# A hybrid decoder layer: operand splits behind the score blocks, chunk states from a bank of their own, the silu at its head's end, and the merge's first products in another order

## What is computed

```python
# mixer A: 12 query heads in 3 groups over 4 key/value heads; windowed, dilated softmax attention
oa = dilated_attention(qa, ka, va)              # groups weighted by their softmax denominators
# mixer B: gated linear attention, 4 heads, chunk by chunk
o_t = q_t S_t ;  S_t = diag(a_t) S_{t-1} + k_t^T v_t
ob = rmsnorm(ob, gn_b) * silu(rb)
# merge
y = sigmoid(ga) * (oa @ w_proj_a) + sigmoid(gb) * (ob @ w_proj_b)
x = x + y @ w_out
# channel mixer
x = x + (silu(h2 @ w_ffn_gate) * (h2 @ w_ffn_up)) @ w_ffn_down      # h2 = rmsnorm(x)
```

## Time and profile before

| what | value |
|---|---|
| median of three runs | 1862.59 us (1861.71 to 1868.87) |
| the profiled execution | 1860.7 us, of which the span is 1859.0 us |
| TensorE busy | 1790.2 us, 96% of the span |
| VectorE, ScalarE, GpSimd busy | 1081.9, 702.9, 487.1 us |
| mean granted TensorE clock | 0.994 of full |
| memory traffic | 150.88 MB read, 44.45 MB written |

### The profile page before, as it was taken

One profiled execution on the slowest core, in us unless ns is written; L12 is line 12 of the kernel. 1 busy time (PEld: TensorE's weight loads), 2 busy tenths in 40 slices (PEclk: granted clock), 3 DMA queues, 4 the chain that ended last, 5 costly groups with the idle time before them and its releaser, 6 DMA issues. The chain is left out here.

```text
span 1859.0 us, 27056 instructions
## 1 busy us (share of the span) xinstructions
PE 1790.2 (96%) x9188; PEld 1518.4 (82%) x9188; DVE 1081.9 (58%) x1928; ACT 702.9 (38%) x1598; POOL 487.1 (26%) x578
## 2 busy tenths in 40 slices
PE   6999999999999999999988999989999999999999
PEld 6888887988887888888876888868888888878887
DVE  4362452643734949485766554596555555556786
ACT  5333243243333335353535213453333333334443
POOL 2010001110114424150602000006665556520120
PEclk9999999999999999999999999999999999999999
DMA  7211321413222111111117323312323223278764
GB/s 204 88 42 59 93 86 50 127 63 86 74 74 79 49 35 49 32 45 45 39 63 249 100 70 114 134 65 97 107 91 122 91 99 105 85 266 311 249 223 168
DMA packets 169294, 196.35 MB, mean 106 GB/s; under 512 B 9552, under 2 KB 119472, under 8 KB 168704
## 3 DMA queue, kind: packets, MB, share of 16 engines
q1 hardware_dynamic: 156816, 163.13, 27.4%
q0 software_dynamic: 6128, 21.74, 3.6%
q10 hardware_dynamic: 6272, 10.49, 1.5%
HBM read 150.88 MB, written 44.45 MB: 105 GB/s over the span
## 5 line engine op out<-in xcount | busy, mean ns | idle before, releaser
L2236 PE MATMUL bank<-act_hi,w_hi 128*128 128x512 f32 x568 | 230.6, 406 | 3.9 <-DVE act_lo L1870 3.6
L2238 PE MATMUL bank<-act_hi,w_lo 128*128 128x512 f32 x568 | 224.1, 395 | 0.0
L2237 PE MATMUL bank<-act_lo,w_hi 128*128 128x512 f32 x568 | 223.6, 394 | 0.0
L2236 PE MATMUL bank<-ca,wq 128*128 128x512 f32 x528 | 206.3, 391 | 7.6 <-DVE wq L1981 5.3
L2238 PE MATMUL bank<-ca,wq 128*128 128x512 f32 x528 | 205.5, 389 | 0.0
L2237 PE MATMUL bank<-ca,wq 128*128 128x512 f32 x528 | 205.5, 389 | 0.0
L2236 PE MATMUL bank<-w_hi,act_hi 128*128 128x256 f32 (+1 forms) x576 | 180.7, 314 | 2.2 <-DVE act_lo L1553 2.2
L2238 PE MATMUL bank<-w_hi,act_lo 128*128 128x256 f32 (+1 forms) x576 | 177.4, 308 | 0.0
L2237 PE MATMUL bank<-w_lo,act_hi 128*128 128x256 f32 (+1 forms) x576 | 177.3, 308 | 0.0
L1537 DVE TENSOR_TENSOR w_lo<-w_raw,w_hi 128x1024 fp32r<-128x1024 f32 x38 | 46.1, 1224 | 154.1 <-ACT w_hi L1002 154.1
L2236 PEld LDWEIGHTS bank<-act_hi,w_hi 128*128 128x128 f32 x568 | 108.5, 191 | 27.4 <-DVE act_lo L1870 4.2
(11 more groups left out here) (357 smaller groups left out, 4222.0 us busy)
## 6 DMA issues: line engine op xcount, KB each, us to landing
w_raw<-in_w_in SPq DMA_DIRECT2D x60, 512.0 KB, 4.1
rawd<-in_w_ffn_down SPq DMA_DIRECT2D x99, 256.0 KB, 5.1
rx<-y_scratch SPq DMA_DIRECT2D x77, 256.0 KB, 4.2
wr<-in_w_ffn_gate SPq DMA_DIRECT2D x11, 1024.0 KB, 5.3
wr<-in_w_ffn_up SPq DMA_DIRECT2D x11, 1024.0 KB, 5.3
y_scratch<-sq SPq DMA_DIRECT2D x11, 1024.0 KB, 4.3
y_scratch<-yq SPq DMA_DIRECT2D x33, 256.0 KB, 2.0
gate_scratch<-gbuf ACTq DMA_DIRECT2D x32, 256.0 KB, 2.0
```

What stands on the lines that cost most here:

```text
L2236: pe.matmul(ps, lhs_hi, rhs_hi, start=first, stop=False, skip_group_check=onto)
L2237: pe.matmul(ps, lhs_hi, rhs_lo, start=False, stop=False, skip_group_check=onto)
L2238: return pe.matmul(ps, lhs_lo, rhs_hi, start=False, stop=last, skip_group_check=onto)
```

## The change

It does five things.

1. **Splits behind score units** (blocks 8 to 15 of each attention head): ScalarE's cast goes behind the block's copies and exponentials, VectorE's subtraction and `merge_mul` behind its score units.
2. **Silu at its head's end**: `act_silu(h)` runs at s=11 of its own head, ahead of that step's jobs; its table is loaded at s=7. ScalarE's loop over the heads is written out in full.
3. **The last chunks**: the products for the states of chunks 4 to 7 go to bank 1, `dve_last_m` updates the state without waiting for ScalarE's square, and chunk 7's product, which nobody reads, is left out.
4. **Splits of the mixers' outputs**: three casts of oa move to s=10 of the last head, the fourth and the cast of tile 2 to its end; one subtraction follows each chunk, and tile 2's comes right after them. The first product waits slice by slice.
5. **The merge's first step**: all four products with w_pa come first, then the four with w_pb; the second half goes to banks 5, 4, 6 and 7, so `down` has one more wait (at d=2).

```diff
@@ banks of the merge @@
-    def mix_base(it, f):
-        return 4 if (it, f) == (NC_IT - 1, 0) else 0
+    def mix_banks(it, f, xh):
+        if (it, f) == (0, 1):
+            return 5 + xh, (4, 7)[xh]
+        b = 4 if (it, f) == (NC_IT - 1, 0) else 0
+        return b + xh, b + 2 + xh
@@ act_head_a @@
-                for k in HI_A.get(s, []):
-                    hi_a(k % 4, 2 * h + k // 4 + 2)
+                if s < 8:
+                    for k in HI_A.get(s, []):
+                        hi_a(k % 4, 2 * h + k // 4 + 2)
...
+                if s >= 8:
+                    for k in HI_A.get(s, []):
+                        hi_a(k % 4, 2 * h + k // 4 + 2)
@@ act_head @@
+                if s == 2 * TB - 1:
+                    act_silu(h)
                 for kind, j, jh in jobs_b(s, h, tail):
...
-                if tail and s == 2:
-                    act_silu(h - 1)
+                if s == 7:
+                    act.preload_act_table_set("silu_and_others")
+                if h == H - 1 and s == 10:
+                    for i in range(3):
+                        split_hi(i)
@@ act_silu @@
             act.activation(g_t[:, :, :], g_t[:, :, :], ACT.Silu).then_inc(g_done, 1)
-            act.preload_act_table_set("natural_log_exp_and_others")
+            if h < H - 1:
+                act.preload_act_table_set("natural_log_exp_and_others")
@@ split_hi and what follows the heads on ScalarE @@
-            if i == 0:
-
+            if i == 1:
+                act.wait_ge(kh_ready, 8 * H - 2)
+            if i == 3:
                 act.wait_ge(kh_ready, 8 * H)
-                act.wait_ge(att_done, 8 * H)
...
+        for h in range(H):
+            act_head(h, h > 0)
+        split_hi(3)
+        hi_tile(2, RC0 + 1)
         for c in range(4, 8):
             act_square(H - 1, c, rest_ps(c))
-            if c < 7:
-                split_hi(2 * (c - 4))
+            if c == 7:
+                split_hi(4)
             act_normed(H - 1, c, rest_ps(c))
             act_t(H - 1, c - 1)
-            if c < 7:
-                split_hi(2 * (c - 4) + 1)
-        split_hi(6)
-        split_hi(7)
-        act_silu(H - 1)
+        split_hi(5)
         act_t(H - 1, 7)
-        for i in range(8, H + 2 * H):
+        for i in range(6, H + 2 * H):
             split_hi(i)
-        hi_tile(2, RC0 + 1)
+        act.preload_act_table_set("sigmoid_and_others")
         leave_phase(act)
         enter_phase(act, 3)
@@ dve_head_a @@
                 if s < 8:
                     qk_norm(s)
                     rope(s)
-                else:
+                for j in UNITS_AT.get(s, []):
+                    dve_unit(j)
+                if s >= 8:
                     for k in HI_A.get(s, []):
                         lo_a(A0 + TA * h + k, k % 4)
                     if behind and s in MUL_AT:
                         merge_mul(h - 1, MUL_AT[s])
-                for j in UNITS_AT.get(s, []):
-                    dve_unit(j)
@@ VectorE, last chunks @@
+        def dve_last_m(c):
+            n = 8 * (H - 1) + c
+            if c < 7:
+                dve.wait_ge(kv_ready, n + 1)
+                dve.wait_ge(state_done, n)
+                dve.scalar_tensor_tensor(out=state[:, (c + 1) % 2, :], in0=state[:, c % 2, :],
+                                         scalar=elast[:, c:c + 1], in1=banks[1][:, 0:DV],
+                                         op0=ALU.mult, op1=ALU.add).then_inc(state_done, 1)
+            dve.wait_ge(o_sq, n + 1)
+            dve.tensor_scalar(ost[:, 1, c:c + 1], ost[:, 0, c:c + 1], 1.0 / DV, EPS,
+                              ALU.mult, ALU.add).then_inc(o_var, 1)
...
         for c in range(4, 8):
-            dve_m(H - 1, c, rest_ps(c))
-            if c > 4:
-                split_lo(2 * (c - 5))
-                split_lo(2 * (c - 5) + 1)
-        split_lo(6)
-        split_lo(7)
+            dve_last_m(c)
+            if c == 4:
+                dve.wait_ge(kh_ready, 8 * H)
+                dve.wait_ge(att_done, 8 * H)
+            split_lo(c - 4)
+        lo_tile(C0 + 2, 2)
+        for i in range(4, 7):
+            split_lo(i)
         dve_gate(H - 1)
-        for i in range(8, H + 2 * H):
+        for i in range(7, H + 2 * H):
             split_lo(i)
-        lo_tile(C0 + 2, 2)
         leave_phase(dve)
@@ merge @@
-            dve.wait_ge(mix_ready, 8 * it + 4 * f + xh + 3)
+            dve.wait_ge(mix_ready, 5 + 2 * f + xh if it == 0 else 8 * it + 4 * f + xh + 3)
@@ TensorE, last chunks @@
+                mm = pe.matmul(ps[:, 0:DV], qh[:, P * c:P * c + P], state[:, c % 2, :], start=False, stop=True)
+            if kv is None or c < 7:
+                mm = pe.matmul(ps[:, DV:2 * DV] if kv is None else kv[:, 0:DV], khat[:, c, :], vtok[:, c, :],
+                               start=True, stop=True)
+            mm.then_inc(kv_ready, 1)
...
         for c in range(4, 8):
-            pe_m(H - 1, c, rest_ps(c), 1 if c > 4 else 0)
+            if c == 4:
+                pe.wait_ge(st_evac, E0 + 2 * TB * H)
+            pe_m(H - 1, c, rest_ps(c), 1 if c > 4 else 0, banks[1])
             if c == 7:
 
-                pe.wait_ge(st_evac, E0 + 2 * TB * H)
-                pe.wait_ge(stage_lo, H)
+                pe_t(H - 1, 6)
                 pe.wait_ge(lo_done, C0 + 1)
-                stream(banks[0], 0, oa_hi, oa_lo, 0, H).then_inc(mix_ready, 1)
-            pe_t(H - 1, c - 1)
-        pe_t(H - 1, 7)
+                stream(banks[0], 0, oa_hi, oa_lo, 0, H, staged=0).then_inc(mix_ready, 1)
+            pe_t(H - 1, c - 1 if c < 7 else 7)
         leave_phase(pe)
@@ TensorE, merge @@
+        def first_mix():
+
+            stream(banks[mix_banks(0, 0, 1)[0]], 0, oa_hi, oa_lo, 1, H).then_inc(mix_ready, 1)
+            for k in (2, 1, 3):
+                pe.wait_ge(lo_done, C0 + k + 1)
+                for xh in range(2):
+                    b = mix_banks(0, k // 2, xh)[k % 2]
+                    if k == 2:
+                        stream(banks[b], k, oa_hi, oa_lo, xh, H).then_inc(mix_ready, 1)
+                    else:
+                        stream(banks[b], k, act_hi, act_lo, xh,
+                               staged=H if k == 1 and xh == 0 else None).then_inc(mix_ready, 1)
...
+                if it == 0 and d == 2:
+                    pe.wait_ge(y_done, 4)
```

More of the change, by code:

```diff
@@ L2238, in three, with stream @@
             return pe.matmul(ps, lhs_lo, rhs_hi, start=False, stop=last, skip_group_check=onto)
-        def stream(ps, k, hi, lo, xh, kts=NK, staged=0, slot=None):
+        def stream(ps, k, hi, lo, xh, kts=NK, staged=None, slot=None):
             slot = slot_of(k) if slot is None else slot
             for kt in range(kts):
-                if staged:
+                if staged is not None:
                     pe.wait_ge(stage_lo, staged + kt + 1)
```

39 lines of the change are left out of this document (16 added, 23 removed).

## The result

| | before | changed |
|---|---|---|
| median of four runs | 1864.89 us (1861.71 to 1868.87) | 1834.51 us (1832.36 to 1836.34) |
| ratio, 95% interval | | 0.9836 (0.9809 to 0.9862) |
| span of the profiled execution | 1859.0 us | 1831.4 us |
| TensorE busy, mean granted clock | 1790.2 us, 0.994 | 1780.8 us, 0.995 |

What follows compares the result with a forecast made beforehand. TensorE, busy 96% of the span, bounds the kernel, so only its waits and half clock can go: 13.5 + 4.5 + 5.0 + 2.6 = 25.6 us off 1860.7 gives 1835.1, stated as 1836 us, range 1827 to 1849.

Steps and rivals of the forecast that it cites:

- Splits behind the score units: Attention: moving VectorE's subtraction and ScalarE's cast removes 9.6 us of `u_t` and 3.9 of `pt` waits, together 13.5 us.
- The clock in attention: Third and fourth attention heads: half-clock stretches of 2.9 and 1.6 us vanish, 4.5 us; bounds 0 and 4.5.
- the bound that a shift of phase brings stretches elsewhere: Attention's half-clock saving: its lower bound, 0 us, if as many half-clock stretches appear elsewhere.
- no window below full clock before 980: Sign expected in the changed kernel's profile: TensorE's clock stays at full in every window before 980 us.
- Silu: Third stage: 4.1 us of normed-output waits and 0.9 of mask waits go, together 5.0 us; bounds 0 and 5.0.
- Last chunks: Last head's chunks: chunk 4 starts 1.4 us later, second token half's product 1.7 earlier; bounds 1.4 lost, 3.5 won.
- Merge's first step: Merge up to `down`: 3.6 us of waits and 2.7 of half clock go; late gates leave 2.6 won, earlier terms included.
- the wait ahead of `down`: Before `down`: TensorE stands 2.9 us for the gates of w=2, then loses 2.7 us at half clock.
- the third stage ends about 3.9 us earlier: End of third stage: last subtraction at 993.5 instead of 996.2, plus 1.2 us of tile 2, so gates come about 1008.6.
- That the gates come in time: Rival at `down`: gates not late, or clock holds; 2.7 to 5.7 us more saved, 1830 us; chance 0.2.
- That the waits move within a block: Rival in attention blocks 13 and 14: half of the 13.5 us stays, plus a 2.9 us half-clock stretch, 1846; chance 0.22.

Runs made afterwards that it cites:

- the silu alone: The kernel before with only the silu moved to its head's end in every head, none behind the last chunks: 1857.30 us, ratio 0.9971.

## Why the prediction was right, and where it was not

- **Splits behind the score units** (13.5 us). The mechanism was right to the row: no `u_t` wait, four `pt` waits of 0.84 to 0.93 us where 0.78 was forecast, no stream waits for a late tile. The size was 16.8 us (4.2 a head: 122.29 to 118.08). The term took a wait at its listed idle time; the three `u_t` waits of a head cost 0.24 us more each, and 3.34 together instead of 2.45. That makes 3.6 us over four heads, and with the `pt` waits worth 3.5 instead of 3.9 the missing 3.3 us.
- **The clock in attention** (4.5 us). In these two profiles the difference came out as forecast (21.2 less 16.8 is 4.4). Part of that is luck: the old attention took 3.1 us longer in another profile, at half clock in all four heads, and the bound that a shift of phase brings stretches elsewhere came true in eleven profiles, with 1.4 to 1.8 us in the third stage, but not in the one that is compared. The changed kernel has a new stretch of its own, behind the transposes' wait of 1.54 us at 950.35, which the forecast "no window below full clock before 980" ruled out. It costs 1.4 us (the next transposes come 4.43 us behind these); in six of the other kernels the same wait of 1.5 us left the clock at full, and they come after 3.0:

```profile
950.66:953.37 2.71, 2.71 (x9) 2.12 (x8) 2.71 (x4) 1.89 (x4) 1.46 (x1) 0.50 0.59 204
```

- **Silu** (5.0 us, and 1.4 given back). Right: 1.9 us a head (a period of 97.2 for 99.1; 1.67 were forecast), 5.7 in three heads, and 392.18 to 387.96 us for the whole stage with the silu alone, neither with a stretch at half clock; and the wait ahead of chunk 4 grew by 1.2 us (0.58 to 1.76).
- **Last chunks** (1.7 us). Right in kind: the run that undoes the chain is 1.9 us longer, 1.5 in the profile, and the transposes follow each other every 2.87 us (950.35 less 947.48), where about 3 were forecast.
- **Merge's first step** (6.3 us saved, the wait ahead of `down` as their price). TensorE came to `down` when forecast: 45.7 us behind chunk 4 (991.45 less 5.98 and 939.74), the working gives 45.4 (1012.3 less 965.45 and 1.4). What failed is the price, in the step "the third stage ends about 3.9 us earlier". VectorE did: its last work ends 26.4 us behind chunk 4 instead of 31.9, 5.6 us less, and the forecast had 3.9 and the 1.4 by which chunk 4 comes later. But the stage ends with the last engine, and that was now GpSimd, 3 us after VectorE. The forecast looked at VectorE alone, since in the kernel before it was the last: there GpSimd issued its two loads 9.5 us ahead of the end of the last subtraction of ob and their last packet moved 2.4 us ahead of it; now they were issued 3.9 us ahead and the last packet came 2.3 us behind. So the wait was 5.98 us and not 2.9. The half clock behind it cost 1.4 us, not 2.7. And of the 6.3 us for the order nothing was won here, since the run that undoes it is no slower; with the gates in time the order was worth 3.
- **The sum**. 1835.1 and the 1.9 us by which the median lay above the profiled execution make 1837.0; the forecast wrote 1836. That is well within the noise, but it brought the number nearer to the result.
- **The rivals**. That the gates come in time was wrong the other way: they were later than forecast. That the waits move within a block did not happen. The measured time, 1.5 us under the forecast, comes from an underrated attention part and an overrated merge, and isn't a proof of either step.

## What to carry to other kernels

When work is taken off the engine that used to reach a barrier last, work out anew which engine is last, and count for each the loads that it has issued itself and must drain. Loads that the barrier need not wait for are better issued by an engine that takes no part in it. Put a bulk load behind the small one that the next step waits for. Move a split for a later step behind what TensorE needs now, on each queue: here that alone gave 17 of 28 us in the profiles and 23 of 30 in the medians. An order of products is worth its waits only if no other wait ends at the same point. Compare two profiles stretch by stretch, and look for half clock in each stretch before a difference is put down to the change.

## What I had not expected of the hardware

- A listed wait of TensorE understates its cost by 0.24 us: 1.55 us for a row of 1.32.
- The granted clock after one and the same wait (2.5 us, behind the same work) was 1.00 in the changed kernel's profile and lower, 0.58 over four microseconds in the one shown, in all eleven others that have part 1 or VectorE's half of it, which cost 1.4 to 1.8 us; after one of 1.5 us it fell in three kernels and stayed at full in six.
- GpSimd's drain behind two loads took until 2.5 to 3 us after VectorE's last subtraction, no matter whether the loads were issued 3.9 or 7.7 us before that end; with no such loads it held nothing, and x followed after 0.36 us.
